# Regrouped matmuls and one shared 128-row operand in the expert stage of a two-layer S5 / Conformer / mixture-of-experts kernel

## What is computed

```python
def moe_swiglu(h, w_router, b_router, w_gate, w_up, w_down):
    logits = (h @ w_router).astype(jnp.float32) + b_router.astype(jnp.float32)
    top_v, top_i = lax.top_k(logits, TOP_K)
    top_w = jax.nn.softmax(top_v, axis=-1)
    gates = jnp.sum(jax.nn.one_hot(top_i, N_EXPERTS, dtype=jnp.float32) * top_w[..., None], axis=-2)
    out = jnp.zeros(h.shape, h.dtype)
    for e in range(N_EXPERTS):
        out = out + gates[..., e:e + 1] * swiglu(h, w_gate[e], w_up[e], w_down[e])
    return out
```

## Time and profile before

| | |
|---|---|
| median of 3 runs | 1790.09 us (1789.62 to 1790.26) |
| the profiled execution's own time | 1790.85 us |
| its span | 1789.1 us |
| TensorE matmul busy | 1706.7 us (95% of the span) |
| VectorE / ScalarE / GpSimd busy | 645.0 / 350.6 / 73.5 us |
| chain that ended last | TensorE 91%, VectorE 4%, ScalarE 3%, DMA 2% |
| moved by DMA | 396.18 MB, mean 221 GB/s |

### The profile page before, as it was taken

How to read it: one execution, slowest core, us unless ns; L and a number is a source line. 1 busy time by engine, 2 the same in 40 slices (tenths; PEclk the granted TensorE clock), 3 DMA queues, 4 the chain that set the end, 5 groups by cost and what they waited for, 6 DMA issues and landing times.

```text
span 1789.1 us, 23244 instructions
## 1 busy us (share of the span) xinstructions
PE 1706.7 (95%) x9661; PEld 878.3 (49%) x9661; DVE 645.0 (36%) x1479; ACT 350.6 (20%) x749; POOL 73.5 (4%) x147
## 2 busy tenths in 40 slices
PE   6999999799999999989988899999999999999996
PEld 3655454288888844437866654343223222322232
DVE  5988961755545404155894520000000000000002
ACT  4324550311111100025373320000000000000001
POOL 2110100000000030000110000000000000000000
PEclk9999999899999999989999799999999999999998
DMA  8414542723332152252433099999999999999992
GB/s 306 149 18 159 194 127 94 226 56 95 95 94 80 44 109 64 88 226 94 119 92 100 0 371 376 372 384 409 343 407 392 409 343 404 389 409 331 408 390 91
DMA packets 194984, 396.18 MB, mean 221 GB/s; under 512 B 34339, under 2 KB 104587, under 8 KB 188730
## 3 DMA queue, kind: packets, MB, share of 16 engines
q1 hardware_dynamic: 189504, 391.23, 60.6%
q0 software_dynamic: 4112, 3.34, 1.2%
q10 hardware_dynamic: 1258, 0.07, 0.0%
HBM read 389.36 MB, written 1.05 MB: 218 GB/s over the span
## 4 chain that ended last, share of the span: by engine, by line
PE 91%; DVE 4%; ACT 3%; DMA 2%; issue 1%; ACTq 0%; DVEq 0%; SPq 0%
PE ps L978 88%; PE ps L981 2%; DMA work<-in_w_ada_dram 1%; DVE rstd L1823 1%; DVE aT L1831 0%; DVE work L1840 0%; ACT dg L671 0%; ACT work L662 0%; ACT work L663 0%; DVE hT L1845 0%; DMA work<-in_conv_b_dram 0%; ACT work L778 0%; DVE aT L2057 0%; ACT std L727 0%; ACT aT L735 0%
## 5 line engine op out<-in xcount | busy, mean ns | idle before, releaser
L978 PE MATMUL ps<-ring,work 128*32 128x256 f32 (+4 forms) x3088 | 545.1, 499 | 1.7 <-ACT work L922 1.1
L978 PEld LDWEIGHTS ps<-ring,work 128*64 128x64 f32 (+2 forms) x3088 | 166.9, 128 | 366.8 <-issue 364.0
L978 PE MATMUL ps<-work,ring 128*128 128x512 f32 (+1 forms) x656 | 237.0, 514 | 1.3 <-DVE work L2139 1.3
L978 PE MATMUL ps<-aT,ring 128*128 128x256 f32 (+1 forms) x800 | 235.2, 443 | 2.9 <-ACT aT L735 2.2
L2277 DVE TENSOR_TENSOR work<-work,ps 128x512 f32<-128x512 f32 (+4 forms) x27 | 19.5, 730 | 586.5 <-PE ps L978 586.5
L978 PE MATMUL ps<-aT,work 128*64 128x512 f32 (+4 forms) x1088 | 210.6, 468 | 0.0
L978 PE MATMUL ps<-work 128*64 128x64 f32 (+8 forms) x1984 | 194.8, 298 | 9.7 <-DVE work L2107 5.0
L978 PEld LDWEIGHTS ps<-aT,ring 128*128 128x128 f32 x800 | 152.4, 192 | 72.4 <-issue 54.4
L978 PEld LDWEIGHTS ps<-work,ring 128*128 128x128 f32 x656 | 124.5, 190 | 106.4 <-issue 98.5
L978 PEld LDWEIGHTS ps<-work 128*64 128x64 f32 (+5 forms) x1984 | 143.1, 155 | 52.2 <-issue 38.9
L978 PEld LDWEIGHTS ps<-aT,work 128*64 128x64 f32 (+2 forms) x1088 | 104.0, 147 | 93.8 <-issue 84.4
(11 more groups left out here) (345 smaller groups left out, 1258.3 us busy)
## 6 DMA issues: line engine op xcount, KB each, us to landing
ring<-in_moe_w_down_dram SPq DMA_DIRECT2D x70, 1024.0 KB, 8.5
ring<-in_moe_w_gate_dram SPq DMA_DIRECT2D x50, 1024.0 KB, 8.2
ring<-in_moe_w_up_dram SPq DMA_DIRECT2D x48, 1024.0 KB, 10.4
ring<-in_w_ada_dram SPq DMA_DIRECT2D x23, 2048.0 KB
ring<-in_moe_w_up_dram SPq DMA_DIRECT2D x32, 768.0 KB, 7.8
aT<-in_moe_w_down_dram SPq DMA_DIRECT2D x18, 1024.0 KB, 8.6
ring<-in_moe_w_gate_dram SPq DMA_DIRECT2D x24, 768.0 KB, 7.3
aT<-in_moe_w_up_dram SPq DMA_DIRECT2D x16, 1024.0 KB, 8.1
```

The costliest lines, as they stand in the source:

```text
L978: return pe.matmul(o, lhs, rhs, start=start, stop=stop)
```

## The change

1. **Matmuls of mid experts are regrouped.** In `project_in` and `project_out` the 32-slot matmuls of two neighbouring blocks are done together, behind the 64-slot matmuls of both (new inner functions `last_slots`). Both blocks are marked used (`block_used`) only there. With three blocks (down of the 768-wide chunk) the third has its own.
2. **Results of a mid expert and of its light partner stand side by side in one operand.** The light partner's two halves are written to the other half of bank 7 (`at_`), so that `yH` holds for each 512 columns 64 rows of the mid expert and 64 of the light one; `gates` lays out `Sg` to match. A spread piece of a mid group has now two matmuls, one of 128 rows and one of 64 rows (`yB`), where it had three of 64. Heavy groups keep theirs.
3. **Two semaphores for the copies.** `y_ready` becomes `y_ready0` and `y_ready1`, one for each 512 columns; `copy_y` on ScalarE and VectorE does the copies in an order that finishes the first half first.
4. **More small VectorE instructions in `gates`** (7 for 4 in each of four sets), and six more behind it, which prepare a second ranking `who2_i` for the second pass. SyncE waits for `routed` 2 before it decides on that pass.

The core of the diff:

```diff
@@ copy_y on ScalarE
-                        last = act.activation(yH.rearrange("p (b n) -> p b n", b=2), ps[:, 5:7, :], ACT.Copy)
-                    else:
-                        act.activation(yH[:, 0:512], ps[:, 5, :], ACT.Copy)
-                        for q in range(2):
-                            last = act.activation(yB[TP * q:TP * q + TP, 256 * (q % 2):256 * (q % 2) + 256],
-                                                  ps[TP * q:TP * q + TP, 6, 0:256], ACT.Copy)
-                    last.then_inc(sem("y_ready"), 1)
+                        for g in range(2):
+                            act.activation(yH[:, 512 * g:512 * g + 512], ps[:, 5 + g, :], ACT.Copy).then_inc(sem(f"y_ready{g}"), 1)
+                        return
+                    for q in range(2):
+                        act.activation(yB[TP * q:TP * q + TP, 256 * (q % 2):256 * (q % 2) + 256],
+                                       ps[TP * q:TP * q + TP, 6, 0:256], ACT.Copy)
+                    for g in range(2):
+                        act.activation(yH[HP * g:HP * g + HP, 512 * g:512 * g + 512], ps[HP * g:HP * g + HP, 5, :], ACT.Copy)\
+                            .then_inc(sem(f"y_ready{g}"), 1)
@@ project_in
+                    def last_slots(n, d):
+                        lhs = [xg[:, 2 * d + j, SLOT0[r] + HP:SLOT0[r + 1]] for j in range(2)]
+                        for j in range(2):
+                            for g in range(w // 256):
+                                last = mm(ps[TP * g:TP * g + TP, bank + 1, 0:256], lhs[j],
+                                          wblock(n)[:, j, 256 * g:256 * g + 256], d + j == 0, 2 * d + j == KC - 1)
+                        last.then_inc(sem("block_used"), 1)
-                                if big(i):
-                                    lhs = xg[:, k, SLOT0[r] + HP:SLOT0[r + 1]]
-                                    for g in range(w // 256):
-                                        last = mm(ps[TP * g:TP * g + TP, bank + 1, 0:256], lhs,
-                                                  b[:, j, 256 * g:256 * g + 256], k == 0, k == KC - 1)
-                        last.then_inc(sem("block_used"), 1)
+                        if heavy(i) or not big(i):
+                            last.then_inc(sem("block_used"), 1)
+                        elif d % 2:
+                            last_slots(n - 1, d - 1)
+                            last_slots(n, d)
@@ project_out
+                                    at_ = HP * (1 - g if r >= NH + NW else g)
+                                    last = mm(ps[at_:at_ + HP, 5 if big(i) else 7, :], hTs[:, i % 2, u, HP * h:HP * h + HP],
                                               b[:, j, 512 * g:512 * g + 512], first, end)
+                        if heavy(i) or not big(i):
+                            last.then_inc(sem("block_used"), 1)
+                        elif d % 2 or d == blocks - 1:
+                            for e in range(d // 2 * 2, d + 1):
+                                last_slots(n - d + e, e)
@@ spread
-                    mm(o, Gt[half, p, tok], yH[half, 0:512], True, False)
-                    mm(o, Gt[half, NE + p - NW, tok], yB[half, :], False, False)
-                    mm(o, Gt[half, NH + p, tok], yL[half, :], False, True).then_inc(sem("spread"), 1)
+                    mm(o, Gt[:, NH * g + p, tok], yH[:, 512 * g:512 * g + 512], True, False)
+                    mm(o, Gt[half, NE + p - NW, tok], yB[half, :], False, True).then_inc(sem("spread"), 1)
@@ copy_y on VectorE
-                    if p >= NW:
-                        for q in range(2, 4):
-                            dve.tensor_copy(yB[TP * q:TP * q + TP, 256 * (q % 2):256 * (q % 2) + 256],
-                                            ps[TP * q:TP * q + TP, 6, 0:256])
-                    dve.tensor_copy(yL, ps[:, 7, :]).then_inc(sem("y_ready"), 1)
+                    if p < NW:
+                        for g in range(2):
+                            dve.tensor_copy(yL[HP * g:HP * g + HP, :], ps[HP * g:HP * g + HP, 7, :]).then_inc(sem(f"y_ready{g}"), 1)
+                        return
+                    dve.tensor_copy(yH[HP:P, 0:512], ps[HP:P, 7, :]).then_inc(sem("y_ready0"), 1)
+                    for q in range(2, 4):
+                        dve.tensor_copy(yB[TP * q:TP * q + TP, 256 * (q % 2):256 * (q % 2) + 256],
+                                        ps[TP * q:TP * q + TP, 6, 0:256])
+                    dve.tensor_copy(yH[0:HP, 512:D], ps[0:HP, 7, :]).then_inc(sem("y_ready1"), 1)
@@ gates, the sets of comparisons
-                                          (o[:, NW:NH].rearrange("p r (d s) -> p r d s", d=2), mid_a),
-                                          (o[:, NH:NE].rearrange("p r (d s) -> p r d s", d=2), light),
+                                          (halves[:, NH:NH + NW], light[:, 0:NW].broadcast_to([P, NW, 2, HP])),
+                                          (halves[:, NW:NH, 0], mid[:, :, 0:HP]),
+                                          (halves[:, NH + NW:NE, 1], mid[:, :, 0:HP]),
+                                          (halves[:, NW:NH, 1], light[:, NW:NH, 0]),
+                                          (halves[:, NH + NW:NE, 0], light[:, NW:NH, 0]),
```

More of the change, by code:

```diff
@@ L192, in hybrid_backbone @@
         who_i = sb("who_i", [P, NE], I32)
+        who2_i = sb("who2_i", [P, NE], I32)
+        far = sb("far", [P, 2])
         most = sb("most", [P, 1])
@@ L1482, in project_out, with last_slots @@
                     if c == 0 and p0 + i // 6:
-                        pe.wait_ge(sem("y_ready"), 2 * (p0 + i // 6))
-                    for d in range(w // 256):
+                        for g in range(2):
+                            pe.wait_ge(sem(f"y_ready{g}"), 2 * (p0 + i // 6))
+                    tiles, blocks = w // P, w // 256
+                    def last_slots(n, d):
+                        for t in (2 * d, 2 * d + 1):
+                            for g in range(4):
+                                last = mm(ps[TP * g:TP * g + TP, 6, 0:256], hTs[:, i % 2, 4 + t % 2, TP * (t // 2):TP * (t // 2) + TP],
+                                          wblock(n)[:, t % 2, 256 * g:256 * g + 256], c == 0 and t == 0, c == NC - 1 and t == tiles - 1)
+                        last.then_inc(sem("block_used"), 1)
+                    for d in range(blocks):
                         pe.wait_ge(sem(f"block_in{n % NBUF}"), 16 * (n // NBUF + 1))
@@ L1488, in project_out @@
                             t = 2 * d + j
-                            first, end = c == 0 and t == 0, c == NC - 1 and t == w // P - 1
-                            h, u = divmod(t, w // 256)
+                            first, end = c == 0 and t == 0, c == NC - 1 and t == tiles - 1
+                            h, u = divmod(t, blocks)
                             for g in range(2):
@@ L1494, in project_out @@
                                 else:
-                                    last = mm(ps[HP * g:HP * g + HP, 5 if big(i) else 7, :], hTs[:, i % 2, u, HP * h:HP * h + HP],
+                                    at_ = HP * (1 - g if r >= NH + NW else g)
+                                    last = mm(ps[at_:at_ + HP, 5 if big(i) else 7, :], hTs[:, i % 2, u, HP * h:HP * h + HP],
                                               b[:, j, 512 * g:512 * g + 512], first, end)
-                            if big(i) and not heavy(i):
-                                for g in range(4):
-                                    last = mm(ps[TP * g:TP * g + TP, 6, 0:256], hTs[:, i % 2, 4 + t % 2, TP * (t // 2):TP * (t // 2) + TP],
-                                              b[:, j, 256 * g:256 * g + 256], first, end)
-                        last.then_inc(sem("block_used"), 1)
+                        if heavy(i) or not big(i):
+                            last.then_inc(sem("block_used"), 1)
+                        elif d % 2 or d == blocks - 1:
+                            for e in range(d // 2 * 2, d + 1):
+                                last_slots(n - d + e, e)
                         n += 1
@@ L2202, in select @@
                     link(tt_(slot_of[:], rel[:], both(slot0[:]), ALU.add))
+                    link(tt_(slot_of[:], slot_of[:], late[:], ALU.add))
+                    link(ts_(late[:], rel[:], float(HP + TP), float(SLOT0[NH] - SLOT0[2]), ALU.is_ge, ALU.mult))
+                    link(ts_(key[:], rank[:], 1.0, None, ALU.is_equal))
+                    link(tt_(late[:], late[:], both(key[:]), ALU.mult))
                 else:
@@ L2215, in gates @@
             def gates(ph):
[L2216 to L2219 removed]
+                light = iota_s[:, SLOT0[NH]:].rearrange("p (r d s) -> p r d s", r=NH, d=1)
+                mid = iota_s[:, SLOT0[NW]:SLOT0[NH]].rearrange("p (r s) -> p r s", r=NM_)
+                mid_b = mid[:, :, HP:].rearrange("p r (d s) -> p r d s", d=1).broadcast_to([P, NM_, 4, TP])
                 for i in range(2):
@@ L2247, in _ @@
             gates(0)
```

(6 more changed lines are left out.)

26 lines of the change are left out of this document (12 added, 14 removed).

## The result

The changed kernel takes 1759.54 us (median of 4 runs, 1757.61 to 1767.02) against 1789.86 us of the kernel before, a ratio of 0.9839 with a 95% interval of 0.981 to 0.9868: about 30 us faster. The forecast was 1757 us, in a range of 1750 to 1773.

A forecast was written before the change was run, and what follows sets the result against it. TensorE was taken as the bound; its path shortens by 49.6 us, then the DMA ends the last down block at 1731. Adding 1789.1 - 1765.3 and 1.0 of tail gives span 1755.8, time 1757 us, range 1750 to 1773.

The forecast's parts named there:

- What bounds the kernel: Expert stage: TensorE's path sets the end; the DMA is only 10.8 us a mid group shorter.
- The price of a change of kind: Mid blocks: each switch between 64-column and 32-column matmul sets costs 0.145 us; regrouping saves TensorE 44.3 us.
- The pieces, 8 x 0.66 us: Mid groups' spread pieces among blocks: two matmuls for three, 2.11 us for 2.77, shorten TensorE's path by 5.3 us.
- The DMA takes over: After the heavy group, transfers at 404 GB/s set the end: last down block at 1731 us against 1765.3, 34 less.
- The late give-back, copies, gates: Buffers returned in pairs, copies before the pieces, extra VectorE gate work: all covered, cost 0.
- The tail, 24.8 us: Behind the last down block: new pieces cannot overlap, 1.7 us allowed for the clock; +1.0 us (0 to 2.5).
- The sum as a whole: Whole kernel: last down block 1731, plus the old remainder and 1.0 us of tail, gives a span of 1755.8 us.
- Rival A: Weight loads: a longer queue brings no rate, the DMA stays at 390 GB/s; 1774 us, chance 0.12.
- B: Mid blocks: runs of 32-column sets do not stream, each boundary keeps 0.145 us; 1763 us, chance 0.09.
- C: Light runs of mid groups: waits for weights drop TensorE's clock to 1.2 GHz; about 1838 us, chance 0.05.
- D: Mid blocks: the gap belongs to each 128 rows, not the change of kind; 1786 us, chance 0.05.
- The landings: Weight loads: nearly all buffers in flight, landing 15 to 25 us from issue; freed loads issued at 0.4 us each.

The follow-up runs named there:

- Half loads: Only the first 128 of 256 rows loaded of each block after the tenth: changed kernel 1748.27 us; kernel before 1793.01 us against 1789.39 us unmodified.
- the ring of 8: Changed kernel with 8 block buffers (NBUF = 8) where it has 10: 1763.26 us in one run.
- the second execution: Profiled execution of the unmodified changed kernel, measured once more: span 1758.1 us; median of those 5 runs 1759.86 us, ratio 0.9825 to the kernel before.

## Why the prediction was right, and where a term was off

**What bounds the kernel: right.** Half loads change nothing in the kernel before (1767.4 for the last down block, 2.1 us of later start included) and take the changed kernel's to 1716.6.

**The price of a change of kind, 0.145 us: right.** A pair takes 5.45 us. TensorE's path is 49.1 us shorter, 49.6 by the sum.

**The pieces, 8 x 0.66 us: right as a price, nothing as a gain**, as the sum had it, since the DMA's path was longer: 5.3 us alone and 5.5 us with half loads (starts taken off), 0 beside the regrouping.

**The DMA takes over: right.** The forecast was 404 GB/s and a last down block at 1731 us; it is at 1735.5 in the profiled execution, with loads that began 1.8 us later than before, and at 1734.1 in the one after it (2.0 later). So 1 to 3 us are left. The rate from 1370 us on was 401, not 404, over 364 us, which is worth 2.7 us; before that it was 398 over 130 us, which costs 1.9 us where the sum had 3 for the standstill. Together 1.6 us: the size that was off. The reason given for 404, a queue that gets longer, has no support: the ring of 8 had a shorter queue and the same 401.

**The late give-back, copies, gates: 0, right.** The first is measured alone, in the kernel before; in the changed one, holding back four blocks at once left the rate at 402. The copies show in the tail as TensorE's wait of 1.46 us for ScalarE (1.67 for VectorE before); among the blocks there is none. The gates' longer way did not show: TensorE turns them 12.9 us after the first load before (1044.33) and 12.9 us after it in the changed kernel (1046.11).

**The tail, 24.8 us: near for most executions by two errors that cancel, wrong for the profiled one.** It takes 24.0, 24.1 and 24.3 us where the clock holds, 29.8 and 29.9 where it falls. The four pieces were put at 7.7 us; at full clock they take 8.5 from the first matmul to the last add (1735.5 to 1744.1 in the second execution). The 1.7 us for the clock were then not paid. The step said "the granted clock falls here (...); I take 1.7 of it", by the row of before. In the kernel before it fell for 3.4 us and came back. In the new pieces it either doesn't fall, or falls and stays. The likeliest execution pays nothing, the rare one 5.8 us.

**The sum as a whole.** Its span was 1755.8 us. The second execution has 1758.1: 2.0 for the start, 1.1 for the last down block, 0.8 less for the tail. The profiled one has 1765.3: 1.8, 2.7 and 5.0. The start's 2 us stood in no term; it moves by 3 us from one execution to the next.

**Rival A** (390 GB/s) fell with 401, **B** (runs do not stream) with 1.87 us for four sets, **C** (the clock falls for weight stops) with a PEclk of 1.00 over 364 us in which TensorE stood for 12.6, **D** with 2.72 us a block. For C the page "TensorE: Matmul & The Clock Gate" of the Trainium skill, section "HAM oscillation — how this bites in real kernels", tells of waits of several microseconds; among the blocks here none was above 1.3 us, and no run shows more. One argument against C was weaker than it sounded, that a loss shows only with long stops such as the tail's: the one stop of the tail before the clock fell was 1.67 us, not far from the 1.3 us of now. That C did not come true is measured; that it could not was never shown.

**The landings: the time was right, the reason in part wrong.** I wrote that nearly all buffers would be in flight and loads would take 15 to 25 us, and that SyncE would issue freed loads at 0.4 us each. They take 16.5 us from 1240 us on and 17.1 from 1370 us on, 20.6 at most, which is nearly seven blocks of 2.56 us and not ten. The ring still holds them in part: from 1370 to 1734 us SyncE's queue waits 98.1 us for TensorE. The rest is SyncE's own instruction, which now takes long (line 512; min, median and max in ns):

```profile
SPq L512 <- PE ps L984: 98.1, 60, 5.1
```
```profile
L512 SPq DMA_DIRECT2D ring<-in_moe_w_up_dram x40: 373/2303/4827, 1385.3 to 1708.6; - x40
L512 SPq DMA_DIRECT2D ring<-in_moe_w_down_dram x37: 372/1817/4718, 1377.3 to 1709.7; - x37
...
DMA to landing us min/median/max: 13.7/17.1/20.6
```

## What to carry to other kernels

Where matmuls of different column groups alternate, count the changes of kind, not the matmuls, and compare a mixed block with a pure one in the same trace: the difference is the price, and sorting the matmuls of two blocks takes most of it away. Before costing such a gain, work out the next bound from the bytes left and the rate at which the trace has its best stretch: here 50 us of TensorE's path were worth 30 us of time, a second edit on the same path nothing, and one buffer more 2 to 3 us. A rate read while TensorE still holds the buffers is TensorE's rate as much as the DMA's, so take the best stretch and not the mean. When the tail of one profiled execution differs from the sum, look at its granted clock and at other executions before explaining it.

## What the runs showed of the hardware, not expected

**Loads in flight.** From 1240 us on the issue of a 1 MB load took 0.37 us (median) in the kernel before. In the changed kernel, with about seven loads under way, the medians are 1.8 to 2.3 us (rows above), and the issue is part of the chain:

```profile
1487.02 2.05 SPq L512
...
1489.26 2.36 SPq L512
...
1491.80 17.12 DMA ring<-in_moe_w_gate_dram
```

I read this as the next issue waiting for an earlier load to finish. The same is seen at the very start of the stage of the kernel before, where no buffer is missing: the first six loads are issued in 0.4 to 0.5 us each, the seventh in 1.35, the eighth to tenth in 2.2 to 2.4 us. With a ring of 8 the medians are back at 0.37 us, with between five and six loads under way. Why seven, no run here tells.

**Rate and length of the queue.** The same loads moved 383 GB/s with about three in flight (8.7 us to landing, 3.4 blocks of 2.56) in the kernel before, 401 with between five and six (ring of 8) and 401 to 407 with nearly seven. In the kernel before a load can start only when TensorE gives a buffer back, and TensorE is the bound, so 383 is the rate at which TensorE takes the blocks; whether so short a queue could move more was not separated. Above five in flight a longer queue brought nothing.

**A clock that falls and stays.** In the last pieces of the new form the granted clock fell in two of eight profiled executions (the first of the changed kernel, and the one with half loads) and then stayed at 1.2 GHz for all of the remaining 12 to 13 us of matmuls, although TensorE had no pause between them. In the old form, whose 64-row matmuls overlap on two halves of the rows, it fell in three of six, each time for 3.4 us, and came back during the same work. The three that fell are the three without the regrouping (the kernel before, with half loads, with the late give-back); the three with it did not fall, so the form of the pieces and what runs before them are not told apart. Nor is a low clock under work new to the pieces. The kernel before has it ahead of the first blocks, behind stops of 4.05 and 2.95 us, with TensorE busy for 16.2 of 17 us:

```profile
1007.00:1017.00 10.00, 9.22 (x43) 9.22 (x44) 7.08 (x25) 4.29 (x10) 0.00 (x0) 0.50 0.00 0
1017.00:1024.00 7.00, 7.00 (x37) 7.00 (x36) 3.16 (x18) 4.93 (x9) 0.00 (x0) 0.52 0.01 2
```

Filling the stop before the tail changed nothing that can be seen, and an execution without any stop for weights had the long tail too. What decides whether it falls, and whether the form of the matmuls keeps it down, stays open: two executions are too few.
